# One buffer in place of two for transposed probabilities, and three evacuations moved from ScalarE to VectorE

## The reference, cut to what matters

```python
q = (rmsnorm(c_q, q_norm_g) @ w_uq)...            # MLA queries: 64 plain + 32 rotary
kv = (rmsnorm(c_kv, kv_norm_g) @ w_ukv)...        # MLA keys (64) and values (64) per head
o_mla = causal_block_attention(q_mla, k_mla, v_mla)
o_dsa = indexed_sparse_attention(q_s, k_s, v_s, q_i, k_i, w_i, topk)   # 128 best keys per query
o = jnp.concatenate([o_mla, o_dsa], axis=-1)
return o @ w_o
# both: s = q k^T * scale, masked; p = softmax(s); out = p @ v, per block of 128 queries
```

## Time and profile before

| | |
|---|---|
| median of three runs | 1771.83 us (1769.8 to 1775.08) |
| profiled execution, its own time | 1775.08 us |
| its span | 1773.2 us |
| PE, DVE, ACT, POOL busy | 96%, 57%, 38%, 33% of the span |
| last evacuation of `Vm` ends | 1227.76 us from the span's start |
| first transpose of the attention | 1235.01 us |
| first product of the output projection | 1335.73 us |

### The profile page before, as it was taken

One profiled execution on the slowest core, in us unless ns is written; L12 is line 12 of the kernel. 1 busy time (PEld: TensorE's weight loads), 2 busy tenths in 40 slices (PEclk: granted clock), 3 DMA queues, 4 the chain that ended last, 5 costly groups with the idle time before them and its releaser, 6 DMA issues.

```text
span 1773.2 us, 21944 instructions
## 1 busy us (share of the span) xinstructions
PE 1705.8 (96%) x8704; PEld 1383.7 (78%) x8704; DVE 1008.4 (57%) x1524; ACT 673.0 (38%) x1029; POOL 591.1 (33%) x203
## 2 busy tenths in 40 slices
PE   7999999999999999899999999998999999999997
PEld 6777788888788888788788878686677788888776
DVE  3255535787878788984464555797973222222123
ACT  5473233333433345344433332415664222222122
POOL 1422014443533342000144342242683344443432
PEclk8999999999999999899999999998999999999999
DMA  5222003335445545344754322112002233332322
GB/s 175 77 95 95 1 25 96 95 95 160 121 115 140 141 126 135 82 117 138 251 185 144 85 82 72 47 43 84 1 1 66 78 95 95 95 95 73 97 84 80
DMA packets 271659, 172.05 MB, mean 97 GB/s; under 512 B 91051, under 2 KB 249990, under 8 KB 271430
## 3 DMA queue, kind: packets, MB, share of 16 engines
q1 hardware_dynamic: 242848, 146.99, 29.1%
q10 hardware_dynamic: 28406, 22.02, 4.0%
q0 software_dynamic: 304, 1.65, 0.3%
HBM read 149.64 MB, written 20.97 MB: 96 GB/s over the span
## 4 chain that ended last, share of the span: by engine, by line
PE 84%; DVE 5%; DMA 5%; ACT 3%; issue 2%; POOL 1%; SPq 1%; ACTq 0%; DVEq 0%; POOLq 0%
PE PS L703 23%; PE PS L704 22%; PE PS L705 22%; DMA ring<-in_s_w_glu 2%; PE PA L986 2%; PE PA L985 2%; PE PA L965 2%; DMA ring<-in_s_w_in 1%; PE PA L899 1%; PE PA L896 1%; PE PS L1234 1%; PE PA L877 1%; PE PS L1246 1%; PE PA L1218 1%; PE PA L1080 1%
## 5 line engine op out<-in xcount | busy, mean ns | idle before, releaser
L2610 POOL TENSOR_TENSOR ring_lo<-ring,ring_hi 128x2048 fp32r<-128x2048 f32 (+2 forms) x93 | 405.6, 4361 | 969.5 <-ACT ring_hi L1356 969.2
L1356 ACT ACTIVATE ring_hi<-ring 128x2048 fp32r<-128x2048 f32 (+2 forms) x123 | 223.9, 1822 | 253.2 <-PE PS L705 172.0
L703 PE MATMUL PS<-U3h,ring_hi 128*128 128x512 f32 x352 | 139.5, 396 | 3.1 <-POOL ring_lo L2610 3.1
L704 PE MATMUL PS<-U3l,ring_hi 128*128 128x512 f32 x352 | 139.9, 397 | 0.0
L705 PE MATMUL PS<-U3h,ring_lo 128*128 128x512 f32 x352 | 138.9, 395 | 0.0
L2570 DVE TENSOR_TENSOR SF<-PS,rs 128x512 f32<-128x512 f32 x22 | 15.2, 691 | 165.2 <-PE PS L705 165.2
L703 PE MATMUL PS<-HT5h,ring_hi 128*128 128x512 f32 x256 | 105.9, 414 | 1.3 <-DVE U L2262 1.3
L704 PE MATMUL PS<-HT5l,ring_hi 128*128 128x512 f32 x256 | 101.9, 398 | 0.0
L705 PE MATMUL PS<-HT5h,ring_lo 128*128 128x512 f32 x256 | 101.9, 398 | 0.0
L1931 DVE TENSOR_TENSOR ring_lo<-ring,ring_hi 128x2048 fp32r<-128x2048 f32 x30 | 85.3, 2857 | 24.0 <-ACT ring_hi L1356 24.0
L2650 POOL TENSOR_TENSOR W<-PW,CZ 128x1024 f32<-128x1024 f32 x11 | 32.1, 2914 | 157.4 <-ACT CZ L1561 142.3
(11 more groups left out here) (484 smaller groups left out, 4331.9 us busy)
## 6 DMA issues: line engine op xcount, KB each, us to landing
ring<-in_gla_w_in SPq DMA_DIRECT2D x20, 1024.0 KB, 5.2
ring<-in_s_w_in SPq DMA_DIRECT2D x16, 1024.0 KB, 5.8
ring<-in_s_w_glu SPq DMA_DIRECT2D x16, 1024.0 KB, 5.8
ring<-in_w_gate SPq DMA_DIRECT2D x22, 512.0 KB, 4.0
ring<-in_w_up SPq DMA_DIRECT2D x22, 512.0 KB, 5.3
ring<-in_w_down SPq DMA_DIRECT2D x16, 704.0 KB, 4.5
ring<-in_w_in SPq DMA_DIRECT2D x9, 1024.0 KB, 5.1
ring<-in_gla_w_out SPq DMA_DIRECT2D x8, 1024.0 KB, 5.7
```

The costliest lines, as they stand in the source:

```text
L703: pe.matmul(dst, w[0], x[0], start=start, stop=False)
L704: pe.matmul(dst, w[0], x[1], start=False, stop=False)
L1356: act.activation(ring_hi[:, n % NSLOT, 0:plan.size[n]], ring[:, n % NSLOT, 0:plan.size[n]], ACT.Copy)\
L2610: pool.tensor_tensor(ring_lo[:, n % NSLOT, at], ring[:, n % NSLOT, at], ring_hi[:, n % NSLOT, at].bitcast(F32), ALU.subtract).then_inc(wlo ...
```

## The change

It has two parts. The first keeps one buffer `PT2`; C(q) now waits for W(q-1) in place of W(q-2). The second moves the three evacuations into `Vm` from ACT to VectorE, behind the last rotation, and lets ACT split the first weights of the output projection between the second and the third key tile.

```diff
-        PT2 = [place("PT20", [P, 2, TPAD], o)[0], place("PT21", [P, 2, TPAD], pvr_off)[0]]
+        PT2, o = place("PT2", [P, 2, TPAD], o)
...
                 ins.then_inc(slot_free[tile.slot], 1)
-            for i, tile in enumerate(tiles["ukvv"]):
-                act.wait_ge(tile_done, tile.t + 1)
-                nb = 2 if i < 2 else 1
-                act.activation(Vm[:, 2 * i:2 * i + nb, :], PS[:, 2 * tile.slot:2 * tile.slot + nb, :], ACT.Copy).then_inc(slot_free[tile.slot], 1)
-            split_weights(tiles["attn_out"][0].loads[0])
+                if i == 1:
+                    split_weights(tiles["attn_out"][0].loads[0])
...
                 act.wait_ge(pT_ps, p + 1)
-                if p >= 2:
-                    act.wait_ge(pv_out_ps, p - 1)
+                if p > 0:
+                    act.wait_ge(pv_out_ps, p)
...
+            for tile in tiles["ukvv"]:
+                i = tile.t - tiles["ukvv"][0].t
+                nb = 2 if i < 2 else 1
+                dve.wait_ge(tile_done, tile.t + 1)
+                dve.tensor_copy(Vm[:, 2 * i:2 * i + nb, :], PS[:, 2 * tile.slot:2 * tile.slot + nb, :]).then_inc(slot_free[tile.slot], 1)
```

More of the change, by code:

```diff
@@ L1246, in with_values @@
                         ins = pe.matmul(PS[h * 64:h * 64 + 64, 2 + p % 2, 2 * P:3 * P], vals[:, j, (2 * hp + h) * 64:(2 * hp + h + 1) * 64],
-                                        PT2[p % 2][:, h, j * P:(j + 1) * P], start=j == 0, stop=j == i + 1)
+                                        PT2[:, h, j * P:(j + 1) * P], start=j == 0, stop=j == i + 1)
                 ins.then_inc(pv_out_ps, 1)
@@ L1806, in copy_transposed @@
                 act.wait_ge(pT_ps, p + 1)
-                if p >= 2:
-                    act.wait_ge(pv_out_ps, p - 1)
+                if p > 0:
+                    act.wait_ge(pv_out_ps, p)
                 n = min(i + 2, 4) * P
-                ins = act.activation(PT2[p % 2][:, :, 0:n], PS[:, 0:2, 0:n], ACT.Copy)
+                ins = act.activation(PT2[:, :, 0:n], PS[:, 0:2, 0:n], ACT.Copy)
                 if i + 2 > 4:
-                    ins = act.activation(PT2[p % 2][:, :, n:n + P], PS[:, 2 + p % 2, 0:2 * P].rearrange("p (h n) -> p h n", h=2), ACT.Copy)
+                    ins = act.activation(PT2[:, :, n:n + P], PS[:, 2 + p % 2, 0:2 * P].rearrange("p (h n) -> p h n", h=2), ACT.Copy)
                 ins.then_inc(pT_sb, 1)
```

## The result

The changed kernel takes 1784.78 us, the median of 13 executions; the kernel before takes 1774.92 beside it. The ratio is 1.0059, with an interval of 1.0047 to 1.0070: 10.5 us slower (8.3 to 12.4), or 9.9 between the two medians. The forecast was 1777.8 us, or +6.0, with a range up to 1780.5. The direction was right and the size too small; the time lies outside the range. Of the 7.0 us between 1777.8 and 1784.78, 3.1 belong to the kernel before: the forecast was added to a median of three executions, 1771.83, and the same kernel has 1774.92 here. The profiled execution of the changed kernel has a time of its own of 1782.56 us and a span of 1780.6.

What follows compares the result with a forecast made beforehand. The prediction took PE, busy for 96% of the span, to bound the kernel. One buffer 4.5 plus moved work 1.5 gave +6.0 us on the median 1771.83, so 1777.8 us, range 1773.0 to 1780.5.

Steps and rivals of the forecast that it cites:

- one for one: Whole attention: a change counts only as it moves PE's going on to the output projection, and then fully.
- One buffer: Attention rounds: C also waits for W of the previous pair; 4.4 us more, called 4.5, bounds 2.2 to 5.5.
- blocks 0 and 1: Early blocks: the single buffer costs 0, as ACT stands in E when W ends; up to 0.4 us.
- block 3, sparse: round: Sparse pairs of block 3: 1.31 + 1.24 + 1.28 + 0.09 = 3.92 us a round, 0.31 more.
- T(31) to the end of W(31): End of the attention: W(30) comes between T(31) and C(31), 1.25 us more than 4.01.
- The moved work: Attention's start: T(1) 0.8 to 1.5 us late; 1.5 us more taken, bounds -0.7 to 2.6.
- The central step: Last rotation: POOL's subtraction meets VectorE's four instructions into Qm, making the rotation 4.4 us late.
- Rival B: Attention's start: VectorE holds POOL off until 1225.53; 2.3 us gained there, total +2.2, 1774.0 us; chance 0.14.
- both slow rounds: First attention rounds: two rounds lost to PE at 1.2 GHz, 2.2 us before, kept in the changed kernel.
- C (the clock back at 2.4 GHz by T(1)): Attention's start: PE at 2.4 GHz by T(1); moved part -0.7, total +3.8, 1775.6 us; chance 0.10.
- D: Pairs with scores: W hides behind E, only the end's 2.2 us remain; total -2.3, 1769.5 us; chance 0.04.
- E: Attention's start: one more round at 1.2 GHz as PE starts later; +1.1, 1778.9 us; chance 0.08.

Runs made afterwards that it cites:

- The kernel with the later rounding: Kernel before, two buffers kept, Vm evacuations on VectorE, first projection weights rounded after the last key tile: 1775.17 against 1775.90 us, ratio 0.9989.
- the waits filled: Changed kernel plus eight unused transposes on PE in each wait for C(29), C(30) and C(31): 1783.01 against 1775.14 us, ratio 1.0044.
- start was filled: Kernel before with two buffers, Vm on VectorE, rounding after the last key tile, 16 unused transposes behind the first three scores: 1771.36 against 1774.65 us, ratio 0.9978.

## Why the prediction was wrong in size

Two steps of the forecast failed. A serial round was sized a tenth of a microsecond too short, so that the one buffer costs 5.8 us and not 4.5; and what follows the attention was put at nothing, "one for one", where the new trace loses 2.9 us more, in two falls of the clock.

**What bounds the kernel.** The forecast has the moment when PE goes on to the output projection move the end of the kernel one for one. L703 comes 7.6 us later (121.89 - 114.29), and the end of the span 10.46. The kernel with the later rounding gains 3.55 at L703 and 2.05 at the end. So the start of the projection decides most of it, but what the clock does behind it is not the same from kernel to kernel.

**One buffer: the mechanism was right, the size was off.** Forecast 4.5, measured 5.8 (93.95 - 88.13, and 5.81 with this part alone). The terms, as the forecast has them:

| term | forecast | measured |
|---|---|---|
| blocks 0 and 1, from O3 | 0 (up to 0.4) | 0.43 in the change, 0.44 with one buffer there only |
| block 2, sparse: round | 3.20 to 3.25 | 3.30 |
| block 2 in all | 0.9 | about 1.2 |
| block 3, sparse: round | 3.92 | 4.02 |
| block 3 in all, up to T(30) | 1.3 | about 1.86 |
| T(30) to T(31) | +0.9 | +1.0 (4.02 against 3.00) |
| T(31) to the end of W(31) | +1.25 | +1.34 (5.35 against 4.01) |

What failed is the size of a round once it is serial. The forecast added T 1.31, W 1.24, C 1.28 and 0.09 for both handovers. The chain reads 1.31, 1.27, 1.30 (1.02 + 0.28) and 0.13: 0.08 from the end of W to the start of C, where before only PE stood behind W, and 0.05 from C to T. C was 1.02 in the earlier trace rows already, and I took 1.00 from a timeline. W is 1.27 where a wait stands behind it and 1.24 where the next group does; that the next group begins inside its last instruction would explain this, and no run tests it. The forecast's terms add up to 4.4 and the measured ones to 5.8. A tenth a round in the ten rounds of blocks 2 and 3 makes 1.0 of these 1.4 us, and blocks 0 and 1, taken as free, 0.4. The MLA pairs of blocks 2 and 3 keep their rounds to 0.01 us, as forecast.

**The moved work.** Forecast +1.5; the trace has +1.8 up to O3 in the change and +2.15 alone. The central step held to a tenth: one meeting of POOL's pass with a VectorE instruction of two SBUF inputs makes it 4.3 us longer (forecast 4.4). The Trainium skill (SBUF — State Buffer, "SBUF: two separate sides") calls this an exclusive lock held for a whole instruction; on this pair of instructions the traces agree, 7.05 us with it and 2.77 without, and on POOL's scaling they differ, as the last section shows. Rival B (POOL waits instead) is out.

Two smaller steps were off and nearly cancel. T(1) was to be 0.8 to 1.5 us late and is 2.76 (+18.43 against +15.67). The third `Vm` copy waits 0.67 us for its tile, which PE computes at 1.2 GHz, and T(1) starts 5.14 us behind R(0), where the forecast had 4.2. I had let T(1) wait for its scaling, but it waits for C(0), and that stands on ACT behind E(2), which waits for R(2), which stands on VectorE behind a selection round. These pieces of the chain of the new kernel show it:

```profile
1234.22 0.57 DVE acc L2470
...
1235.04 0.20 DVE PB L2536
1235.29 0.91 ACT PB L1798 x4
1236.22 0.60 ACT PT L1807
...
1236.87 1.11 PE PS L1234 x4
```

The other way, the forecast kept both slow rounds of before; the new profile has one less of them, and 0.98 of the 2.76 is regained by O3. How many there are is not fixed: with no edit in this place, one buffer alone had one less than before.

**What the sum did not have.** The clock behind the attention. The forecast priced PE's new waits as waits and looked for the clock only at the start, where it had seen it fall in the earlier trace rows. The same question was there to be asked at the end: the waits behind T(30) and T(31) are new. The price is 1.4 us (7.08 against 5.70) in three of four profiles; in the one profile with the waits filled it is not there. The later fall costs the new kernel another 1.5 us. It is in the kernels with two buffers too, and whether it is the change's doing or one profile's luck for the kernel before stays open.

**The account.** In the profiles 1.8 up to O3, 5.8 for one buffer, 1.4 for the clock at the end of the attention and 1.5 for the later fall make 10.5 us, and the second profile of the change has 10.4. The times show 10.5 (8.3 to 12.4). The first three, 9.0, are put down to the change by the experiments; the last 1.5 are seen in the trace, and their cause is not shown. The parts alone add up to 0.50% in the times against 0.59%, within the intervals.

**The rivals.** C (the clock back at 2.4 GHz by T(1)) is out: the granted clock is 0.50 from 1230 to 1240 in the new kernel; its price, forecast as 2.2 us for two rounds, was 1.5 up to O3 in the one kernel whose start was filled. D is out by block 3's rounds. E, one more slow round at the start, did not come either; there was one less.

## What to carry to other kernels

- When a second buffer goes, the price is read from the pairs where the stage that it hid was last already: 0.4 us in the 16 pairs of blocks 0 and 1, paced by other engines, none in the MLA pairs of blocks 2 and 3, whose scores are longer than C, and 5.4 in the sparse ones, 2.4 of that in the drain of the pipeline, where nothing is left to fill with. Take each serial piece with its whole last instruction and both handovers, here 0.13 us a round.
- Before work is moved earlier, look at what it meets in its new place. Here the same rounding, moved two key tiles further, turned a loss of 2.2 us at L703 into a gain of 3.6 in the trace (at the end of the span, a loss of 3.6 into a gain of 2.1).
- Each new wait of PE's is also a question to the clock, and costs once as a wait and perhaps again as slow products behind it. Follow two traces from a common mark to the end of the span, not only to the end of the changed stretch.

## What the runs showed of the hardware

- Not every POOL operation holds VectorE. The subtraction into `ring_lo` did so in each meeting that I read with an instruction of two SBUF inputs, to about 0.5 us past its own end (1225.58 and 1226.14 in the new kernel). Yet POOL's scaling (L2665, 128x528) ran back to back while VectorE did four of its L2542, which multiply two SBUF tensors, and each kept its 0.73 us. There the hold goes the other way: a scaling takes 1.60 us, also where an L2542 begins inside it, but the three that begin inside a running L2542 take 2.08, 1.69 and 1.92, longer where more of it was still to run (0.61, 0.21 and 0.45 us). All twelve profiles have these three. Rows of the kernel before, POOL and then DVE:

```profile
1301.22 2.08 POOL L2665 TENSOR_SCALAR PB<-PB,mx 128x528 f32<-128x528 f32 x1 [2.47 <-DVE mx L2521]
1311.60 1.60 POOL L2665 TENSOR_SCALAR PB<-PB,mx 128x528 f32<-128x528 f32 x1
```

```profile
1301.10 0.73 DVE L2542 SCALAR_TENSOR_TENSOR XT<-XT,pv,rs 128x512 f32<-128x512 f32 x1
1312.12 0.73 DVE L2542 SCALAR_TENSOR_TENSOR XT<-XT,pv,rs 128x512 f32<-128x512 f32 x1
```

- The clock of PE falls and comes back without a difference that these traces show. With the same 2.46 us of work in five it fell in one kernel and not in another; with the same wait of 3.07 us it fell in ten profiles and not in two; and starts that differ only in the buffer, which changes nothing up to T(2), differ by a whole round (O3 at 26.16 and 25.10, 22.60 and 23.70). Executions of the kernel before ran from 1768.65 to 1784.13 us on one chip. Over these 29 the time goes with the mean granted clock, which lay between 0.979 and 0.986 (correlation -0.93). With the start filled they lay within 6.4 us (1767.24 to 1773.68), without within 9.9 (1769.97 to 1779.82).
